# Moving 40 modulation blocks of a two-block transformer kernel: 9 beside the projections, 21 in the attention, 3 behind each of three norms, one behind the first MLP tiles

## The chip, the cores and the metric

One core of a Trainium2 chip. The metric is the device time of one execution in microseconds (us). The five engines are named as in the profile: PE (TensorE, with PEld for its weight loads), DVE (VectorE), ACT (ScalarE), POOL (GpSimd) and SP (SyncE, which here only issues transfers).

## What is computed

The reference runs two blocks on 256 latent tokens (and, in the first block, 256 context tokens) of width 1024, in float32. Only the first block's first two layers matter here. In each of them, for both kinds of tokens:

```python
mod = silu(c) @ w_mod[i] + b_mod[i]          # 6 chunks of 1024, for c and for c_ctx
h = modulate(rms_norm(x, norm1_g[i]), mod[0], mod[1])
x = x + mod[2] * mixer_i(h)                  # differential attention, then neighbourhood attention
x = x + mod[5] * squared_relu_mlp(modulate(rms_norm(x, norm2_g[i]), mod[3], mod[4]), w_mlp1[i], w_mlp2[i])
```

The modulation is one product per layer of a vector pair (the two condition vectors) with a 1024 x 6144 matrix. Behind these two layers come two layers of the second block (gated MLPs, three attention branches, memory attention), which the change leaves as they are.

## The kernel before

**Three passes for each product.** A weight block comes by DMA into one of three slots of `ring`. ACT rounds it to `Wh` and DVE takes the rest `Wl` (`prepare`, lines 1550 and 2076; each in two halves of 128x1024, into one of two buffers), and PE multiplies high by low, low by high and high by high (`passes`, line 806). One step of 128 output rows over 1024 inputs is 24 matmuls. A slot is free for the next transfer once DVE has split it.

**The modulation.** 48 blocks of 1024x256 weights, unsplit. The first 8 (scale and shift of the first norm) are streamed at the start. The other 40 pass through the same ring, 1 MB each, and are used raw: `modulation_block` (line 960) does 8 products with 32 columns of `cT` (shown as 16 records) and accumulates in one PSUM bank, `mod_sum`, which is the last bank of pool A. Here the slot is free once PE has used it. After a group of blocks ACT copies `mod_sum` (`copy_group`), PE folds it (`fold_group`), ACT copies that (`copy_folded`) and DVE adds the bias into `MOD` (`add_group`). Before the change the 40 are placed so: one in each of the 20 steps of layer 0's projections (`first_layer`, `next_modulation(j)`), and 20 in the attention of layer 0, at steps 0, 1, 3, 5 and 6 of every eight (`modulation_step`). Steps are counted from 0; PE does what belongs to step s in its round s + 1.

**The order of transfers** is one list, `blocks`, written in `first_weights`; SP walks through it and waits, for each entry, for the slot of the entry three places back. In layer 0 a projection block is followed by two modulation blocks; after the last projection block come the 20 of the attention, then the four of `a_w_o`. `OUT_SPLITS` has ACT split the first two of these in its rounds 30, 31, 33 and 35 of the attention (32 units, so 35 rounds on PE).

**A norm.** The squares of the 8 tiles of `XT` are summed by POOL and PE; ACT takes a root (lines 1608, 1610), DVE refines it, and then for each of 8 tiles DVE makes `TMP` (line 2167), ACT rounds it to `HTh` (line 1594), DVE takes `HTl` (line 2174), and PE starts on that tile (`side_by_side`: two output tiles at once, 6 matmuls for each k). While that chain starts up, PE has nothing. The weights of the first two output tiles are split long before; of the next block, the first half is split ahead of the norm (`prepare((0,))`) and the second behind it (ACT inside `norm` with `rest=True`, DVE after the 8th tile).

**Pools.** Pool A has PSUM banks pa0 to pa3, pool V pv0 to pv3. A uses three while `mod_sum` is in use: up to the second norm of layer 0. From there it uses four.

**End of the value projections.** The attention's first product waits until the last two value tiles are copied out. In layer 0 the fourth value tile is in pool V and copied by DVE (line 2058), in layer 1 all are in pool A and copied by ACT.

Of the kernel before, what the change touches and what calls it, by code (L numbers as in the profile page):

```python
# [45 lines left out]
QK_MOD = 20  # L46
# [52 lines left out]
def constant_pack():  # L99
# [10 lines left out]
    put("ones", np.ones((P, S)))  # L110
# [17 lines left out]
    put("minus", -np.ones((P, P)))  # L128
# [11 lines left out]
    qc, kc = p % GRID_W, t % GRID_W  # L140
    start = np.clip(qc - NA_COLS // 2, 0, GRID_W - NA_COLS)
    inside = (kc[None, :] >= start[:, None]) & (kc[None, :] < start[:, None] + NA_COLS)
    back = p // GRID_W * GRID_W + GRID_W - 1 - qc
    put("ncol", np.where(inside, 0.0, NEG)[back])
    half = HEAD // 2
    freq = np.power(np.float32(10000.0), -np.arange(half, dtype=np.float32) * np.float32(2.0 / HEAD)).astype(np.float32)
    put("freq", freq[p % half][:, None])
# [6 lines left out]
LATE_CONST = CONST["minus"][0]  # L154
# [159 lines left out]
def program(nc, I, out):  # L314
    ctx = ExitStack()
    with ctx:
# [92 lines left out]
        modtwo = big(12288, 2, 256)  # L409
        cT = big(12800, KT, 64)  # L410
        fold = BIG[:, 13312:13344]
        modt = big(13344, 2, 64)
# [84 lines left out]
        const_late = sem("const_late")  # L497
        mod_in = [sem(f"mod_in{k}") for k in range(KT)]
# [90 lines left out]

        def first_weights(i):  # L590
            w = I["a_w_qkv" if i == 0 else "b_w_qkv"][0]
            if i == 0:
                later = [columns_of_modulation(m) for m in range(LATER_MOD)]
                columns(w, 0, 256)
                for n in range(12):
# [5 lines left out]
                    for src, c in later[2 * n:2 * n + 2] if n < 8 else later[8 + n:9 + n]:  # L601
                        columns(src, c, 256, False)
                for src, c in later[QK_MOD:]:
                    columns(src, c, 256, False)
            else:
                by_columns(w, 0, 2 * D)
                for c in range(2):
                    halves_of_rows(w, 2 * D + c * 512, 512)
            by_columns(I["a_w_o" if i == 0 else "b_w_o"][0], 0, D)
            if i == 1:  # L610
                late_bias.append(len(blocks))
            n = CHUNK * P
            for c in range(FF1 // n + 1):
                if c < FF1 // n:
# [56 lines left out]
        late_bias = []  # L671
# [94 lines left out]
        def _(pe):  # L766
# [342 lines left out]
            def near_attention(tag):  # L1109

                for s in range(len(NEAR_STEPS) + 3):
# [17 lines left out]
                    if s >= 3:  # L1129
# [5 lines left out]
                        for k in range(4):  # L1135
                            for m in range(2):
# [3 lines left out]
                                   v_full if k == 3 and m else None)  # L1140

            def first_layer(i):
                if i == 0:
                    modulation(0)
                else:
                    norm(("n1", i), ALL)
                tiles = qk_tiles(i)
                order = len(tiles)
                for j in range(order + 2):
# [30 lines left out]
                    if i == 0:  # L1180
                        next_modulation(j)
                for n in range(2, 4):
                    values_half(value_tiles(i, 1), CTX_TOKS + LAT_TOKS, 512, n - 2)
                    if i == 0:
                        next_modulation(order + n)
# [34 lines left out]
                if i == 0:  # L1220
                    pe.wait_ge(mod_copied, len(MOD_GROUPS))
                    A.width = BANKS
                norm(("n2", i), tc)
                for c in range(FF1 // P // CHUNK + 1):
# [1659 lines left out]
```

## Time and profile before

| | us |
|---|---|
| median of 3 runs | 2632.49 (2631.89 to 2634.2) |
| profiled execution, its own time | 2634.66 |
| its span | 2632.9 |
| PE busy | 2505.2 (95%) |
| DVE busy | 1702.4 (65%) |
| ACT busy | 1233.6 (47%) |
| POOL busy | 234.2 (9%) |
| mean granted TensorE clock | 0.983 of full |
| mean of DMA | 150 GB/s |

Busy times are of the span. A row of the timeline gives the start, the duration, engine, line, operation, output and inputs, and in brackets the idle time of that engine before it with what ended it. Layer 0 of the first block runs until about 737 us, layer 1 from there to about 1200 us.

### The profile page before, as it was taken

The page shows a single profiled execution, that of the slowest core. Times are in us where ns is not written, and L with a number is a line of the kernel's source. Part 1 is how long each engine was busy: PE and PEld are TensorE (multiplying, and loading weights), DVE is VectorE, ACT ScalarE, POOL GpSimd, SP SyncE. Part 2 cuts the span into 40 slices and gives each one's busy share as a digit, 9 for nine tenths or more (in the row PEclk, how much of TensorE's full clock was granted, in tenths as well). Part 3 has the DMA queues.
Part 4 walks back from the last instruction along what each step waited for, and adds up shares of the span by engine and source line. Part 5 has one row for each costly group of instructions (what it writes and reads, how often), then busy time and mean ns, then how long its engine had stood idle before and what let it go on. Part 6 is the DMA issues. An engine that isn't in the chain of part 4 may idle for free.

```text
span 2632.9 us, 41678 instructions
## 1 busy us (share of the span) xinstructions
PE 2505.2 (95%) x16875; PEld 2220.0 (84%) x16875; DVE 1702.4 (65%) x3155; ACT 1233.6 (47%) x2226; POOL 234.2 (9%) x277
## 2 busy tenths in 40 slices
PE   6999989999989999999999999999999999999998
PEld 4666578888877689999989979899899899798997
DVE  4664855455575566677656777776676567777765
ACT  3443743323255554454444455554544444555543
POOL 1000010000053320000010012000000100120001
PEclk9999999999989999999999999999999999999999
DMA  7655723323235335556555425465765554254654
GB/s 273 201 176 183 234 80 109 97 99 96 96 87 122 81 99 165 172 160 178 168 167 157 149 89 163 141 177 165 199 183 168 167 156 149 88 167 138 177 167 138
DMA packets 497439, 393.74 MB, mean 150 GB/s; under 512 B 26216, under 2 KB 464752, under 8 KB 496352
## 3 DMA queue, kind: packets, MB, share of 16 engines
q1 hardware_dynamic: 494448, 384.92, 48.1%
q0 software_dynamic: 2080, 3.53, 1.1%
q8 instruction: 134, 2.20, 0.4%
q10 hardware_dynamic: 720, 2.62, 0.3%
q14 instruction: 57, 0.47, 0.1%
HBM read 389.99 MB, written 1.05 MB: 149 GB/s over the span
## 4 chain that ended last, share of the span: by engine, by line
PE 82%; DVE 10%; ACT 3%; DMA 2%; issue 2%; POOL 1%; SPq 0%; DVEq 0%; ACTq 0%
PE pv L806 35%; PE pa L806 30%; PE pv L1298 6%; PE pv L771 4%; PE pv L1297 3%; DVE Wl L2076 3%; DMA ring<-in_a_w_qkv_dram 2%; PE pa L771 2%; ACT Wh L1550 2%; PE pa L776 1%; PE pa L960 1%; DVE HTl L2083 0%; POOL BIG L2804 0%; DVE TMP L2167 0%; DVE HTl L2061 0%
## 5 line engine op out<-in xcount | busy, mean ns | idle before, releaser
L2076 DVE TENSOR_TENSOR Wl<-ring,Wh 128x1024 fp32r<-128x1024 f32 (+4 forms) x688 | 758.3, 1143 | 267.9 <-ACT Wh L1550 264.8
L1550 ACT ACTIVATE Wh<-ring 128x1024 fp32r<-128x1024 f32 (+4 forms) x688 | 641.0, 979 | 499.1 <-PE pv L806 329.9
L806 PE MATMUL pa<-HTl,Wh 128*128 128x256 f32 (+1 forms) x1648 | 540.5, 328 | 38.0 <-DVE HTl L2174 24.0
L806 PE MATMUL pv<-HTl,Wh 128*128 128x256 f32 (+1 forms) x1872 | 539.0, 288 | 16.1 <-DVE T L2513 5.8
L806 PE MATMUL pv<-HTh,Wh 128*128 128x256 f32 (+1 forms) x1872 | 537.2, 287 | 0.0
L806 PE MATMUL pv<-HTh,Wl 128*128 128x256 f32 (+1 forms) x1872 | 537.2, 287 | 0.0
L806 PE MATMUL pa<-HTh,Wl 128*128 128x256 f32 (+1 forms) x1648 | 522.2, 317 | 0.0
L806 PE MATMUL pa<-HTh,Wh 128*128 128x256 f32 (+1 forms) x1648 | 521.9, 317 | 0.0
L806 PEld LDWEIGHTS pa<-HTl,Wh 128*128 128x128 f32 x1648 | 320.8, 195 | 72.0 <-issue 45.5
L806 PEld LDWEIGHTS pv<-HTl,Wh 128*128 128x128 f32 x1872 | 359.7, 192 | 21.7 <-issue 12.2
L806 PEld LDWEIGHTS pv<-HTh,Wl 128*128 128x128 f32 x1872 | 359.8, 192 | 2.5
L806 PEld LDWEIGHTS pv<-HTh,Wh 128*128 128x128 f32 x1872 | 359.7, 192 | 2.5
L806 PEld LDWEIGHTS pa<-HTh,Wl 128*128 128x128 f32 x1648 | 320.9, 195 | 20.4 <-issue 1.4
L806 PEld LDWEIGHTS pa<-HTh,Wh 128*128 128x128 f32 x1648 | 320.3, 194 | 18.5
L1298 PE MATMUL pv<-HID,Wh 128*128 128x512 f32 x704 | 246.8, 398 | 0.0
L2743 POOL TENSOR_TENSOR Pb<-Pb 128x256 f32<-128x256 f32 (+1 forms) x60 | 62.6, 1044 | 1453.7 <-ACT Pb L1561 1452.8
L1297 PE MATMUL pv<-HID,Wl 128*128 128x256 f32 x672 | 189.2, 282 | 0.0
L806 PE MATMUL pv<-HID1l,Wh 128*128 128x512 f32 (+1 forms) x512 | 172.0, 336 | 0.0
L806 PE MATMUL pv<-HID1h,Wl 128*128 128x512 f32 (+1 forms) x512 | 172.0, 336 | 0.0
L806 PE MATMUL pv<-HID1h,Wh 128*128 128x512 f32 (+1 forms) x512 | 172.0, 336 | 0.0
L2204 DVE SCALAR_TENSOR_TENSOR XT<-pv,MOD,XT 128x256 f32<-128x256 f32 x216 | 95.7, 479 | 112.0 <-PE pv L806 111.2
L1298 PEld LDWEIGHTS pv<-HID,Wh 128*128 128x128 f32 x704 | 130.4, 188 | 29.4
(288 smaller groups left out, 3307.3 us busy)
## 6 DMA issues: line engine op xcount, KB each, us to landing
ring<-in_ffn_w_gu_dram SPq DMA_DIRECT2D x176, 512.0 KB, 5.1
ring<-in_w_mlp_dram SPq DMA_DIRECT2D x64, 1024.0 KB, 5.4
ring<-in_ffn_w_down_dram SPq DMA_DIRECT2D x64, 704.0 KB, 4.6
ring<-in_w_in_dram SPq DMA_DIRECT2D x42, 1024.0 KB, 5.2
ring<-in_w_mod_dram SPq DMA_DIRECT2D x40, 1024.0 KB, 5.6
ring<-in_a_w_qkv_dram SPq DMA_DIRECT2D x12, 1024.0 KB, 5.3
ring<-in_b_w_qkv_dram SPq DMA_DIRECT2D x12, 1024.0 KB, 5.3
ring<-in_w_out_dram SPq DMA_DIRECT2D x8, 1024.0 KB, 5.1
```

The source lines that it names most:

```text
L771: m = nc.tensor.matmul(o, lhsT=lhsT, rhs=rhs, start=start, stop=stop)
L776: m = nc.tensor.transpose(o, x, C("ident"))
L806: m = nc.tensor.matmul(o, lhsT=x, rhs=y, start=first and j == 0, stop=last and j == 2)
L960: m = nc.tensor.matmul(mod_sum[32 * j:32 * j + 32, 0:256], lhsT=cT[:, k, 30 - 2 * at:62 - 2 * at], rhs=w[:, k, :], start=at == 0 and k < 4 ...
L1297: nc.tensor.matmul(b[:, 0:S], lhsT=wl[:, k, :], rhs=HID2h[:, kk, :], start=False, stop=False)
L1298: m = nc.tensor.matmul(b.rearrange("p (a n) -> p a n", a=2), lhsT=wh[:, k, :], rhs=HID2[:, :, kk, :], start=kk == 0, stop=kk == 2 * half - 1)
L1550: ins = nc.scalar.activation(Wh[rows, p % SPLIT, a:b], ring[rows, i % RING, a:b], ACT.Copy)
L2076: ins = v.tensor_tensor(Wl[rows, p % SPLIT, a:b], ring[rows, i % RING, a:b], Wh[rows, p % SPLIT, a:b].bitcast(F32), ALU.subtract)
L2204: m = v.scalar_tensor_tensor(XT[:, k, half], b[:, at:at + S], MOD[:, i, gate * KT + k, w:w + 1], XT[:, k, half], ALU.mult, ALU.add)
L2743: nc.gpsimd.tensor_tensor(a, a, squares(k)[:, 0:N], ALU.add).then_inc(sum_ready, 1)
```

## The change

Names and line numbers below are those of the new kernel where they are quoted from the diff. It does five things.

1. **Places.** `QK_PLACES` gives 9 modulation blocks to the projections of layer 0 (steps 0, 2, ..., 12, 15, 17, ahead of the rotation product of that step), `modulation_step` now gives 21 to the attention, 3 stand behind the norm product of (n2, 0), of (n1, 1) and of (n2, 1), and the last one behind the first two MLP tiles of layer 1. The list of transfers follows: each trio stands behind the first weight block of its stage.
2. **Splits.** Ahead of those norms nothing of the second weight block is split any more (`last=()`); its first half is split amid the tiles, between the 4th and the 5th, by ACT (`shifted`) and DVE (`normed`), and its second half behind the 8th, by both.
3. **Groups.** Five groups instead of four (8, 16, 8, 12, 4 blocks); the fourth is copied, folded and added in the neighbourhood attention of layer 1, the fifth in the first chunks of its MLP. So `mod_sum` stays in use, and pool A has three banks up to chunk 1 of that MLP. The gains of the last norm are made after the neighbourhood attention.
4. **Value tile.** In layer 1 the fourth value tile is now in pool V too and copied by DVE.
5. **Room.** The small modulation buffers move into the place of late constants; of these, 257 columns are loaded in the projections and 1408 in the MLP of layer 1 (before: 1793 in the projections).

```diff
-QK_MOD = 20
+QK_PLACES = (0, 2, 4, 6, 8, 10, 12, 15, 17)
+QK_MOD = len(QK_PLACES)
+DIFF_MOD = 21
+HOLE_MOD = 3
...
-    return n if QK_MOD <= n < LATER_MOD else None
-MOD_GROUPS = ((0, FIRST_MOD), (FIRST_MOD, 16), (FIRST_MOD + 16, 16), (FIRST_MOD + 32, 8))
-MOD_COPIED = {18: 2, 32: 3}
-MOD_FOLDED = {0: 1, 18: 2, 34: 3}
-MOD_ADDED = {2: 1, 23: 2, 36: 3}
+    return n if QK_MOD <= n < QK_MOD + DIFF_MOD else None
+AFTER_DIFF = QK_MOD + DIFF_MOD
+AFTER_MLP = AFTER_DIFF + HOLE_MOD
+LAST_MOD = AFTER_MLP + HOLE_MOD
+MOD_GROUPS = ((0, FIRST_MOD), (FIRST_MOD, 16), (FIRST_MOD + 16, 8), (FIRST_MOD + 24, 12), (FIRST_MOD + 36, 4))
+MOD_COPIED = {10: 1, 23: 2}
+MOD_FOLDED = {10: 1, 23: 2}
+MOD_ADDED = {15: 1, 28: 2}
+NEAR_COPIED, NEAR_FOLDED, NEAR_ADDED = 2, 4, 6
...
-                    for src, c in later[2 * n:2 * n + 2] if n < 8 else later[8 + n:9 + n]:
-                        columns(src, c, 256, False)
-                for src, c in later[QK_MOD:]:
-                    columns(src, c, 256, False)
+                    for at, place in enumerate(QK_PLACES):
+                        if n == (place // 2 if place < 16 else place - 8):
+                            modulation_columns(at, at + 1)
+                modulation_columns(QK_MOD, AFTER_DIFF)
+                by_columns(I["a_w_o"][0], 0, D)
...
+                elif c == 0:
+                    by_columns(I["w_mlp1"][i], 0, 256)
+                    first = LAST_MOD if i else AFTER_DIFF
+                    modulation_columns(first, first + HOLE_MOD)
+                    by_columns(I["w_mlp1"][i], 256, n)
+                    if i:
+                        modulation_columns(LAST_MOD + HOLE_MOD, LATER_MOD)
...
-            return [(V if i == 0 and t == 3 else A, ("v", i, c, t)) for t in range(4)]
+            return [(V if t == 3 else A, ("v", i, c, t)) for t in range(4)]
...
+                    if i == 0 and j in QK_PLACES:
+                        next_modulation(QK_PLACES.index(j))
                     if j >= 2 and i == 0:
                         pe.wait_ge(qn_ready, seen.more(qn_ready))
...
-                    if i == 0:
-                        next_modulation(j)
...
                 norm(("n2", i), tc)
+                first = LAST_MOD if i else AFTER_DIFF
+                for n in range(first, first + HOLE_MOD):
+                    next_modulation(n)
...
             def shifted(shift, tcols, layer):
                 for k in range(KT):
+                    if k == KT // 2 and (shift, layer) != (0, 0):
+                        prepare((0,))
...
-                    square_block(("o", i), n, 2, tc)
-                norm(("n2", i), tc, RS, 3, layer=i, rest=True)
+                    square_block(("o", i), n, 2, tc, ())
+                norm(("n2", i), tc, RS, 3, layer=i)
+                prepare((1,))
...
-            def normed(terms, shift):
+            def normed(terms, shift, split=True):
                 for k in range(KT + 1):
+                    if k == KT // 2 and split:
+                        prepare((0,))
...
-                for _ in range(4 if i else 1):
-                    prepare()
+                if i:
+                    for _ in range(3):
+                        prepare()
+                    copy_in(value_tiles(i, 0)[3][1], Va[:, 3, 0:512], lambda b: b[:, 0:512])
+                prepare()
+                copy_in(value_tiles(i, 1)[3][1], Va[:, 3, 512:D], lambda b: b[:, 0:512])
```

How this moves instructions, at three places. First, DVE around the second norm of layer 0, before (XT is the residual, T_71 a scratch tile):

```order
L2204 SCALAR_TENSOR_TENSOR XT<-pv,MOD,XT 128x256 x4
L2076 TENSOR_TENSOR Wl<-ring,Wh 128x1024
L2157 SCALAR_TENSOR_TENSOR T_71<-RS 128x512
L2158 SCALAR_TENSOR_TENSOR T_71<-pa,T_71 128x512
L2160 SCALAR_TENSOR_TENSOR RS<-T_71,RS 128x512
L2167 SCALAR_TENSOR_TENSOR TMP<-XT,AM,RS 128x256 x4
L2174 SCALAR_TENSOR_TENSOR HTl<-TMP,MOD,HTh 128x256 x2
L2167 SCALAR_TENSOR_TENSOR TMP<-XT,AM,RS 128x256 x2
```

and now:

```order
L2259 SCALAR_TENSOR_TENSOR XT<-pv,MOD,XT 128x256 x4
L2210 SCALAR_TENSOR_TENSOR T_71<-RS 128x512
L2211 SCALAR_TENSOR_TENSOR T_71<-pa,T_71 128x512
L2213 SCALAR_TENSOR_TENSOR RS<-T_71,RS 128x512
L2222 SCALAR_TENSOR_TENSOR TMP<-XT,AM,RS 128x256 x4
L2229 SCALAR_TENSOR_TENSOR HTl<-TMP,MOD,HTh 128x256 x2
L2222 SCALAR_TENSOR_TENSOR TMP<-XT,AM,RS 128x256 x2
L2229 SCALAR_TENSOR_TENSOR HTl<-TMP,MOD,HTh 128x256 x2
L2222 SCALAR_TENSOR_TENSOR TMP<-XT,AM,RS 128x256 x2
L2229 SCALAR_TENSOR_TENSOR HTl<-TMP,MOD,HTh 128x256 x2
L2129 TENSOR_TENSOR Wl<-ring,Wh 128x1024
L2222 SCALAR_TENSOR_TENSOR TMP<-XT,AM,RS 128x256 x2
```

The half split has moved from ahead of the root to the middle of the tiles, in front of the 5th `TMP` and of the 4th `HTl`. Second, DVE between the last projection step and the first scores (L2313, L2370) of layer 1, before:

```order
L2377 SCALAR_TENSOR_TENSOR BIG<-BIG,gq,RQ 128x512
L2076 TENSOR_TENSOR Wl<-ring,Wh 128x1024 x8
L2313 ISA Lb,mx<-pv,con 128x256
```

and now:

```order
L2436 SCALAR_TENSOR_TENSOR BIG<-BIG,gq,RQ 128x512
L2129 TENSOR_TENSOR Wl<-ring,Wh 128x1024 x6
L2111 COPY BIG<-pv 128x512
L2129 TENSOR_TENSOR Wl<-ring,Wh 128x1024 x2
L2111 COPY BIG<-pv 128x512
L2370 ISA Lb,mx<-pv,con 128x256
```

The two copies of the value tile are new on DVE, and the second stands behind a whole block's split. Third, the last rounds of layer 0's attention on PE, before (con,Pb are the turned probabilities, BIG,PT the products with the values, con,Oa a finished head turned):

```order
L960 MATMUL pa<-ring,BIG 32x256 x8
L776 MATMUL pa<-con,Pb 128x128 x4
L771 MATMUL pa<-BIG,PT 128x128 x4
L776 MATMUL pa<-con,Pb 128x128 x2
L771 MATMUL pa<-BIG,PT 128x128 x4
L776 MATMUL pa<-con,Oa 128x128 x4
L776 MATMUL pa<-con,Pb 128x128 x2
```

and now:

```order
L990 MATMUL pa<-ring,con 32x256 x8
L806 MATMUL pa<-con,Pb 128x128 x4
L801 MATMUL pa<-BIG,PT 128x128 x4
L806 MATMUL pa<-con,Pb 128x128 x2
L801 MATMUL pa<-BIG,PT 128x128 x4
L806 MATMUL pa<-con,Oa 128x128 x4
L990 MATMUL pa<-ring,con 32x256 x8
L806 MATMUL pa<-con,Pb 128x128 x2
```

There is one modulation block more, in PE's round 33, and so each of the `a_w_o` blocks stands one place later in the list of transfers.

## Rows read from the trace of the kernel before

**Rows 1.** Chain that ended last, 62 to 97 us: start, us, what.
```profile
57.90 5.76 DMA ring<-in_a_w_qkv_dram
...
63.68 2.01 ACT Wh L1550 x2
...
71.60 1.87 PE pa L960 x16
73.46 7.21 PE pa L806 x24
...
81.53 0.43 PE pv L771 x2
81.96 1.00 PE pa L960 x16
82.96 5.67 PE pa L806 x24
```

**Rows 2.** Timeline of PE: its waits at the places of the change.
```profile
70.38 1.22 PE L771 MATMUL pv<-BIG,con 128*128 128x256 f32 x2 [3.01 <-DVE BIG L2377]
...
184.46 1.22 PE L771 MATMUL pv<-BIG,con 128*128 128x256 f32 x2 [4.65 <-DVE BIG L2377]
...
326.22 1.16 PE L771 MATMUL pa<-BIG,PT 128*128 128x128 f32 x8 [1.25 <-ACT PT L1627]
...
385.15 0.76 PE L806 MATMUL pa<-HTl,Wh 128*128 128x512 f32 x1 [6.48 <-DVE HTl L2174]
...
744.83 0.55 PE L806 MATMUL pa<-HTl,Wh 128*128 128x256 f32 x1 [5.90 <-DVE HTl L2174]
...
880.34 1.13 PE L771 MATMUL pv<-BIG 64*128 64x512 f32 x4 [0.89 <-ACT BIG L1627]
...
968.78 0.55 PE L806 MATMUL pa<-HTl,Wh 128*128 128x256 f32 x1 [4.43 <-DVE HTl L2174]
```

**Rows 3.** Timeline of DVE, end of layer 0's value projections.
```profile
235.25 0.69 DVE L2058 COPY BIG<-pv 128x512 f32<-128x512 f32 x1 [20.36 <-PE pv L806]
```

**Rows 4.** Timeline of SP and ACT near the end of layer 0's attention.
```profile
319.59 0.37 SPq L2843 DMA_DIRECT2D ring<-in_a_w_o_dram  x1
...
322.00 1.05 ACT L1550 ACTIVATE Wh<-ring 128x1024 fp32r<-128x1024 f32 x1
```

**Rows 5.** DMA issues, 300 to 330 us: count, KB each, median us to landing.
```profile
ring<-in_a_w_o_dram SPq DMA_DIRECT2D x4, 1024.0 KB, 5.2
```

**Rows 6.** Timelines of ACT and DVE, second norm of layer 0.
```profile
387.66 0.91 ACT L1594 ACTIVATE HTh<-TMP,MOD 128x256 fp32r<-128x256 f32 x2 [0.80 <-DVE TMP L2167]
...
389.25 0.88 DVE L2174 SCALAR_TENSOR_TENSOR HTl<-TMP,MOD,HTh 128x256 fp32r<-128x256 f32 x2
...
396.42 1.23 DVE L2076 TENSOR_TENSOR Wl<-ring,Wh 128x1024 fp32r<-128x1024 f32 x1
...
398.25 0.60 ACT L1627 ACTIVATE XQ<-pa 128x512 f32<-128x512 f32 x1 [2.85 <-PE pa L806]
```

**Rows 7.** Timelines around the norms of layer 1: DVE, SP, ACT, DVE, ACT.
```profile
751.97 1.23 DVE L2076 TENSOR_TENSOR Wl<-ring,Wh 128x1024 fp32r<-128x1024 f32 x1
...
960.46 0.37 SPq L2843 DMA_DIRECT2D ring<-in_w_mlp_dram  x1
...
970.11 0.51 ACT L1594 ACTIVATE HTh<-TMP,MOD 128x256 fp32r<-128x256 f32 x1 [0.41 <-DVE TMP L2167]
...
974.90 1.23 DVE L2076 TENSOR_TENSOR Wl<-ring,Wh 128x1024 fp32r<-128x1024 f32 x1
...
976.90 0.38 ACT L1627 ACTIVATE XQ<-pa 128x256 f32<-128x256 f32 x1 [2.62 <-PE pa L806]
```

**Rows 8.** Stretch 890 to 932: PE, PEld, DVE, ACT, POOL busy, PEclk, DMA share, GB/s.
```profile
890.00:932.00 42.00, 41.28 (x352) 25.94 (x350) 34.77 (x149) 32.38 (x77) 21.76 (x29) 0.97 0.28 44
```

**Rows 9.** Timeline of DVE behind layer 1's value projections.
```profile
881.06 2.36 DVE L2076 TENSOR_TENSOR Wl<-ring,Wh 128x1024 fp32r<-128x1024 f32 x2 [8.94 <-ACT Wh L1550]
```

**Rows 10.** Timeline of ACT in layer 1's attention: the copies of turned probabilities.
```profile
900.83 1.06 ACT L1627 ACTIVATE SQ<-pa 128x512 f32<-128x512 f32 x2
```

More of the change, by code:

```diff
@@ L109, in constant_pack @@
     put("ident", np.eye(P))
-    put("ones", np.ones((P, S)))
+    put("ones", np.ones((P, P)))
     put("block", (p[:, None] // HEAD == p[None, :] // HEAD) * 1.0)
@@ L126, in constant_pack @@
     put("eps", np.full((P, 1), EPS))
-    put("minus", -np.ones((P, P)))
+    t = np.arange(S)
+    qc, kc = p % GRID_W, t % GRID_W
+    start = np.clip(qc - NA_COLS // 2, 0, GRID_W - NA_COLS)
+    inside = (kc[None, :] >= start[:, None]) & (kc[None, :] < start[:, None] + NA_COLS)
+    back = p // GRID_W * GRID_W + GRID_W - 1 - qc
+    put("ncol", np.where(inside, 0.0, NEG)[back])
+    half = HEAD // 2
+    freq = np.power(np.float32(10000.0), -np.arange(half, dtype=np.float32) * np.float32(2.0 / HEAD)).astype(np.float32)
+    put("freq", freq[p % half][:, None])
     pb = np.zeros((P, P))
@@ L408, in program, with spare @@
         posi = over("posi", [P, S], where["BIG"] + 4 * 12032, I32)
[L409 to L412, printed above, removed]
+        def spare(at, tiles, width):
+            return con[:, LAST_CONST + at:LAST_CONST + at + tiles * width].rearrange("p (t n) -> p t n", n=width)
+        modtwo = spare(0, 2, 256)
+        cT = spare(512, KT, 64)
+        modt = spare(1024, 2, 64)
+        fold = con[:, LAST_CONST + 1152:LAST_CONST + 1184]
         MODW = over("MODW", [P, 2048], where["SQ"])
@@ L497, in program @@
         const_late = sem("const_late")
+        const_last = sem("const_last")
         mod_in = [sem(f"mod_in{k}") for k in range(KT)]
@@ L588, in columns_of_modulation, with modulation_columns @@
             return I["w_mod"][layer], n * 256
+        def modulation_columns(m0, m1):
+            for m in range(m0, m1):
+                src, c = columns_of_modulation(m)
+                columns(src, c, 256, False)
         def first_weights(i):
@@ L1146, in first_layer @@
                     norm(("n1", i), ALL)
+                    for n in range(AFTER_MLP, LAST_MOD):
+                        next_modulation(n)
                 tiles = qk_tiles(i)
@@ L1232, in first_layer @@
                             linear(A, ("up", i), c * CHUNK + j, (0, P), ht(tc), N, c == 0 and j == 0)
+                            if i and (c, j) == (0, 0):
+                                for n in range(LAST_MOD + HOLE_MOD, LATER_MOD):
+                                    next_modulation(n)
+                        if i and c == 1:
+                            fold_group(4)
+                            A.width = BANKS
                     if c:
@@ L1573, in square_block @@
                         square(k, tcols, (key, k))
-                    prepare(last)
+                    if last:
+                        prepare(last)
                 else:
@@ L1734, in first_layer @@
                 else:
-                    norm(("n1", i), ALL, RS, 0, mean=PT[:, 1, :], layer=i, rest=True)
+                    norm(("n1", i), ALL, RS, 0, mean=PT[:, 1, :], layer=i)
+                    prepare((1,))
                 tiles = qk_tiles(i)
@@ L1801, in first_layer @@
                             rounded(HID1h[:, c % 2, j, 0:N], TMP[:, j % 2, 0:N])
+                        if i and c == 0:
+                            copy_group(4)
+                        if i and c == 1:
+                            copy_folded(4)
                     if c == FF1 // P // CHUNK and i == DEPTH - 1:
@@ L2182, in norm_mod @@
                          RS[:, half.start - tcols.start:half.start - tcols.start + S]) for half, w in halves(tcols)],
-                       lambda k, half: MOD[:, i, 3 * which * KT + k, (half != LAT):(half != LAT) + 1])
+                       lambda k, half: MOD[:, i, 3 * which * KT + k, (half != LAT):(half != LAT) + 1], key != ("n1", 0))
             def normed_quarters(tcols, gain, r, at, tiles=range(KT)):
@@ L2207, in residual_gated @@
                     if (k + 1) % per_block == 0:
-                        prepare(last if k == KT - 1 else (0, 1))
+                        parts = last if k == KT - 1 else (0, 1)
+                        if parts:
+                            prepare(parts)
             def residual(keys, factor, tiles=range(KT), per_block=0):
@@ L2355, in first_layer @@
                 else:
-                    gains(1, 0, 1)
+                    gains(1, 0)
                     v.tensor_copy(gq[:, 5:6], gq[:, 4:5]).then_inc(am_ready, 1)
@@ L2401, in first_layer @@
                     near_attention(("att", i))
+                    gains(1, 1)
                     N, tc = S, LAT
-                residual_gated(lambda k: (("o", i), k), i, 2, tc, 2, last=(0,))
+                residual_gated(lambda k: (("o", i), k), i, 2, tc, 2, last=())
                 norm_mod(("n2", i), tc, 1, i)
@@ L2419, in first_layer @@
                             rest(HID1h[:, c % 2, j, 0:N], HID1l[:, c % 2, j, 0:N], t)
+                        if i and c == 1:
+                            add_group(4)
                     if c == FF1 // P // CHUNK and i == DEPTH - 1:
@@ L2425, in first_layer @@
                         residual_gated(lambda k: (("dn", i, c - 1), k), i, 5, tc, 4,
-                                       last=(0,) if c == FF1 // P // CHUNK else (0, 1))
+                                       last=() if c == FF1 // P // CHUNK else (0, 1))
             def scaled(name, l, k):
```

55 lines of the change are left out of this document (29 added, 26 removed).

## Prediction

> **What bounds the kernel now.** The table of engines comes first: PE is busy for 2505.2 of 2632.9 us, DVE for 1702.4. So the time is PE's work plus its 128 us of waits, and an instruction elsewhere counts only where PE waits for it. The chain that ended last says it again: nearly all of its time is on PE [rows 1]. In it one modulation block is 1.00 us of PE where the clock is full, and 1.87 behind a wait. The list of PE's waits shows where the change could act [rows 2]: 3.01 in the second projection step, 4.65 in the third pair, 1.25 near the end of layer 0's attention, and 6.48, 5.90 and 4.43 at the three norms. The timelines of DVE, ACT and SP say what ends each wait [rows 3, 4, 6, 7, 9, 10].
>
> The 40 blocks cost PE 40 us in either kernel. The change can gain only where a block falls into a wait of PE, and where something is late no more; and it can lose where the new order makes something late.
>
> **The change part by part**, against the profiled execution (2634.66).
>
> 1. *Projections.* 20 blocks become 9: 11 x 1.00 = -11.0 [rows 1].
> 2. *First wait.* The chain runs through a weight transfer issued at 57.90 only, because its slot comes free behind two modulation blocks; it takes 5.76, ACT's rounding 2.01, and PE waits 3.01 for DVE's query tile behind that [rows 1, 2]. Then PE works at half clock: 1.22 for 0.43, 1.87 for 1.00, 7.21 for 5.67, together 3.2 more [rows 1, 2]. With one modulation block between two weight blocks instead of two, that weight block takes the slot of a weight block which DVE has split long before, so it lands in time. -3.0 and -3.2, so -6.2. Bounds: -6.2 and 0 (the query's own chain of copies stays). I take the whole, since the transfer is the last thing that ended.
> 3. *Second wait.* The 4.65 at 184.46 [rows 2] is the root and the product of the last query tile, behind which PE has nothing queued in either order: 0.
> 4. *End of the value projections.* The modulation block of the last step covered DVE's copy of a value tile (0.69, done at 235.94) [rows 3]. PE now stands at it: +0.9 with the handing over. Bounds 0.7 to 1.0.
> 5. *Attention.* The 21st block stands in PE's round 33, next to the wait of 1.25 at 326.22 [rows 2]: between 0 (it fills it) and +1.0; one fold with its copy and sum has left the attention (ACT and DVE time, bounds -0.8 and 0). I take 0 for both together.
> 6. *The output weights.* They stand one place later in the list of transfers. The first output block gets the place that the second has now, issued at 319.59 [rows 4]. Landing takes 5.2 [rows 5], so it is there at 324.8, and ACT wants the first block at 322.00, in front of copies that PE waits for: +2.8. PE's clock falls in a wait of such length, as in part 2 (where 3.01 brought 3.2): I take +1.2, since part of the wait lies in one that is there already. Bounds for the two together: 0 (ACT gets there later too) and 2.8 + 3.2 = 6.0; I take 4.0. The Trainium skill, "DMA: Bandwidth & Descriptors", section "Anatomy of one DMA — SWDGE (gpsimd) path", gives about 2.0 us and the bytes by 436 GB/s, so an estimated 4.4 us for 1 MB, for another issuing path than SP's; by that the wait would be 2.0 and the sum 0.8 lower. The row has 5.2, and the sum goes by the row.
> 7. *Norms, the blocks.* Three blocks are 3.0 us of PE, and the waits are 6.48, 5.90 and 4.43 [rows 2]. The loads are early: at the last norm the third block's slot comes free where now a weight block is issued at 960.46 [rows 7], and with 5.2 it has landed at 965.7, while PE, whose wait begins at 968.78 - 4.43 = 964.35, comes to the third block at 966.4. So 9 blocks for 0, bounds 0 and +2. The last one, behind the first MLP tiles, is in the open: +1.0.
> 8. *Norms, the split.* Ahead of the norm the half split was covered by the wait. Amid the tiles it isn't: at (n2, 0) ACT ends the 4th `HTh` at 388.57, the half `Wh` takes 1.05 [rows 4], then the half `Wl` 1.23, until 390.9, where DVE takes the next `TMP` now ahead of the 4th `HTl` of 389.25, at about 388.4 [rows 6]. So the tiles behind come 2.5 later, the 8th at 398.9 instead of 396.4 (the end of the last `HTl` is where `Wl` starts now). PE was some 1.0 behind there (it ends the first output tile at 398.25, three matmuls into the 8th tile, while DVE had ended at 396.4), so +1.6. At (n2, 1) DVE ended at 974.90 and the first output tile at 976.90 [rows 7]: PE was 1.2 or so behind, +1.5. There the second weight block may land just when ACT wants it (the 4th `HTh` ends at 970.6), bounds 1.0 and 2.7. At (n1, 1) I have no such lag, +1.9. Together +5.0, bounds 3 and 7.
> 9. *Layer 1's value tiles.* The second copy (0.69) on DVE stands behind a block's split that now starts at 881.06 and takes 2.36 [rows 9], so it ends near 883.9, if the split starts where it does now, 0.3 sooner if not. PE starts at 880.34 [rows 2], but what waits in fact is DVE: its first scores come behind the same split already, and are 0.7 of copy and some handing over later. I take +1.5, bounds 0.7 and 3.6 (all of 883.9 - 880.34).
> 10. *Fourth group* in the neighbourhood attention: PE's fold and DVE's sums, +0.7, bounds 0 and 1.5; PE is busy 41.28 of 42 us there [rows 8]. Its copies are on ACT, busy 32.38 of 42: 0.
> 11. *At nothing:* the fifth group, the gains made later and the late constants' transfer lie beside PE's work in the MLP; their cover is DVE's and ACT's idle fifth. Pool A with three banks was enough for layer 0. If that cover is gone, see rival 3.
>
> Sum: -11.0 - 6.2 + 0.9 + 0 + 4.0 + 1.0 + 5.0 + 1.5 + 0.7 = **-4.1**, so 2630.6 against 2634.66. That execution was 2.2 above the median of the three runs, so against the median 2628.4; I say 2628.5.
>
> A measurement of this kernel can tell about 0.2%, 5.3 us. So the likeliest case is, narrowly, no change that can be told.
>
> **Rivals.**
>
> 1. *As summed*, -4: each uncertain term near its value. For it: each has a row. The sum lies near the limit of what can be told.
> 2. *The new waits are shorter than summed* (faster). In part 6 ACT may come to the split later than at 322.00, since the 21st block and later copies push it, and then nothing waits: -4.0. In part 8 the tile chain could be absorbed more at the last norm; in part 9 only the lower bound may hold, -0.8. Together -9 or so: 2623.5. Against it: the slot's time in part 6 is tied to PE's use of modulation blocks, which would be later too.
> 3. *Pool A with three banks* (slower). In layer 1's attention PE's products of a step take banks of pool A while ACT copies the turned probabilities out, 2 copies in 1.06 us [rows 10]. With one bank less the product of a step must wait for a copy of the step before. I see about 0.4 us of slack now. The stretch is 16 steps and PE has no reserve there (41.28 of 42) [rows 8]: from 0.25 us a step on it outweighs the gain of 4.1, and a whole copy (0.53) and its handing over, 1.0 less the slack, would be 16 x 0.6 = +9.6: then 2638.1, just slower by what can be told (2637.8). For it: ACT's 32.38 of 42. Against it: layer 0 lives with three.
> 4. *The first wait stays* (the change does not do there what it says). If the query tile is late for another reason than the transfer (the three steps of copy, root and product behind PE's own work), 6.2 stay: +2.1, 2634.7 against the median. Against it: at 63.68 ACT's rounding waits for the transfer, and nothing else ends there.
>
> **How the numbers follow.** As summed, no change that can be told, 0.40; faster by more than 5.3 us (rival 2, and the part of case 1 that falls beyond the limit) 0.42; rival 4 0.09, told as the same; rival 3 0.09. So faster 0.42, same 0.49, slower 0.09. The range takes in rival 2 with part 8 at its lower bound (2621), case 1 and rival 4 with a little above (2636): what is left out is rival 3 and some of the best cases. Between faster and same the profile does not decide much; I give the value of the sum, 2628.5.
>
> **What will show it.** In the list of PE's waits: the 3.01 of the second projection step gone and the stretch of 72 to 82 us at full clock (part 2, rival 4); a wait of about 0.9 at the end of the value projections (4); one of some 3 us near round 30 of the attention, ended by ACT behind a transfer (6; rival 2 if it isn't there); at the norms waits of 3.5, 3 and 1.5 us behind three blocks instead of 6.48, 5.90 and 4.43 (7), and new ones in the middle of the tiles, on the 5th tile's `HTl`, of 1 to 2 us (8); before layer 1's attention a gap of over 0.89 ended by DVE's copy (9); in that attention waits of the products for `SQ` copies, once per step (rival 3). Granted clock below 0.9 in stretches without a wait ahead of them would upset all of this. I am wrong in kind if PE's busy time changes by more than the fold and the clock explain, or if the time at the norms falls by 3 us each.

## The result, and the profile after

The changed kernel takes 2641.71 us (median of 7 executions, 2637.8 to 2643.55), the kernel before 2633.3 in the same comparison (7 executions). The ratio is 1.0027 [1.0018, 1.0037]: it is slower, where no change that can be told was forecast, and outside the range (2621 to 2636). The profiled execution is the shortest of the seven, 3.9 us under their median: 2637.8, span 2636.0. Busy times have hardly moved: PE 2505.3 (2505.2 before), DVE 1704.1, ACT 1232.2, POOL 238.7 (234.2 before).

PE's timeline at the places of [rows 2] (start, duration, engine, line, operation, in brackets the wait ahead and what ended it):

```profile
168.10 1.22 PE L801 MATMUL pv<-BIG,con 128*128 128x256 f32 x2 [4.42 <-DVE BIG L2436]
216.51 1.99 PE L801 MATMUL pv<-BIG 64*128 64x512 f32 x8 [0.99 <-DVE BIG L2111]
308.63 1.65 PE L801 MATMUL pa<-BIG,PT 128*128 128x128 f32 x6 [2.91 <-ACT PT L1672]
371.52 0.47 PE L836 MATMUL pa<-HTl,Wh 128*128 128x512 f32 x1 [3.75 <-DVE HTl L2229]
378.86 0.50 PE L836 MATMUL pa<-HTl,Wh 128*128 128x512 f32 x1 [1.32 <-DVE HTl L2229]
733.38 0.35 PE L836 MATMUL pa<-HTl,Wh 128*128 128x256 f32 x1 [3.58 <-DVE HTl L2229]
739.17 0.39 PE L836 MATMUL pa<-HTl,Wh 128*128 128x256 f32 x1 [1.38 <-DVE HTl L2229]
873.34 2.08 PE L801 MATMUL pv<-BIG 64*128 64x512 f32 x4 [4.40 <-DVE BIG L2111]
960.64 0.36 PE L836 MATMUL pa<-HTl,Wh 128*128 128x256 f32 x1 [1.34 <-DVE HTl L2229]
966.50 0.50 PE L836 MATMUL pa<-HTl,Wh 128*128 128x256 f32 x1 [3.14 <-DVE HTl L2229]
```

All that was looked for is there: no wait in the second projection step (the granted clock of 72 to 82 us is 1.00, before 0.77), 0.99 at the end of the value projections, 2.91 near the end of the attention, the three holes down to 3.75, 3.58 and 1.34, a second wait amid the tiles of each norm, and 4.40 ahead of layer 1's attention. So the places tell nothing of a loss. To find it, lay the same matmul of both traces side by side and take the difference of its starts (of its ends, where the row says "end"). That is PE's lead (negative: the changed kernel is ahead):

| place (before, after) | lead |
|---|---|
| first attention's same product (239.68, 219.84) | -19.8 |
| head norm at its end (333.99, 320.29) | -13.7 |
| first tile of (n1, 1) (744.83, 733.38) | -11.5 |
| end of layer 1's value products (879.45, 868.94) | -10.5 |
| end of that attention (938.62, 930.85) | -7.8 |
| end of an output block amid layer 1's MLP (1030.08, 1026.33) | -3.8 |
| 1367.19, 1362.43 | -4.8 |
| 1570.82, 1567.04 | -3.8 |
| 1707.29, 1706.60 | -0.7 |
| 2623.91, 2626.76 | +2.9 |

Up to 1367 us the changed kernel is ahead by about what the sum gave (-4.1). All is lost in the second block, which the change leaves as it is: 1.0 us up to 1571, 3.1 between 1571 and 1707, 3.5 in the rest. What differs there is on POOL, in its products with `before`, a mask of zeros and ones, 512 columns wide, in the constants `con`. First the kernel before, then the changed one: its groups with this mask (busy, mean ns of one), and PE's waits for them (us in total, times, longest):

```profile
L2809 POOL TENSOR_TENSOR TMP<-TMP,con 128x512 f32<-128x512 f32 x10 | 11.2, 1120 | 9.0 <-ACT TMP L1939 8.9
L2804 POOL TENSOR_TENSOR BIG<-BIG,con 128x512 f32<-128x512 f32 x10 | 10.9, 1092 | 388.8 <-DVE BIG L2604 388.8
...
PE pv L771 <- POOL BIG L2804: 9.1, 8, 1.8
```

```profile
L2874 POOL TENSOR_TENSOR TMP<-TMP,con 128x512 f32<-128x512 f32 x10 | 13.1, 1307 | 10.2 <-ACT TMP L1992 10.2
L2869 POOL TENSOR_TENSOR BIG<-BIG,con 128x512 f32<-128x512 f32 x10 | 12.7, 1267 | 389.4 <-DVE BIG L2669 389.4
...
PE pv L801 <- POOL BIG L2869: 11.5, 10, 2.1
```

PE behind the last of these waits in this part of the block, and behind a wait for DVE 50 us later, which is equally long in both; before, then after:

```profile
1570.82 1.56 PE L771 MATMUL pv<-BIG,con 128*128 128x256 f32 x6 [1.54 <-POOL BIG L2804]
1620.78 0.36 PE L806 MATMUL pv<-HTl,Wh 128*128 128x256 f32 x1 [2.70 <-DVE T L2513]
```

```profile
1567.04 2.64 PE L801 MATMUL pv<-BIG,con 128*128 128x256 f32 x6 [1.72 <-POOL BIG L2869]
1618.60 0.55 PE L836 MATMUL pv<-HTl,Wh 128*128 128x256 f32 x1 [2.70 <-DVE T L2578]
```

And PE's clock behind both (columns as in [rows 8]), before and after:

```profile
1570.00:1580.00 10.00, 9.18 (x63) 8.24 (x63) 4.66 (x8) 2.04 (x5) 2.90 (x3) 1.00 0.28 80
1618.00:1640.00 22.00, 19.30 (x161) 19.25 (x161) 19.99 (x34) 12.95 (x23) 7.22 (x7) 1.00 0.54 175
```

```profile
1566.00:1578.00 12.00, 10.96 (x64) 9.71 (x65) 4.85 (x9) 2.25 (x5) 3.50 (x3) 0.86 0.22 68
1618.00:1638.50 20.50, 19.90 (x153) 19.93 (x154) 17.04 (x29) 11.97 (x21) 4.82 (x5) 0.92 0.56 172
```

The same 20 products take 0.18 us more each. The change drops 256 columns of constants ahead of the mask and moves the 256 of `ncol` and the single column `freq` there, so the mask starts at column 1667 of `con`, not 1666. This is part 5 of the change (its "room"), on which the prediction has no word but "at nothing".

### The profile page after: what moved, and what is told of

The parts are those of the page before. It is cut to its first block, busy times and chain, and to the rows that moved or that the text cites. A ratio compares the mean times of both kernels' runs of the same rounds, so it can differ in the third digit from the quotient of the medians.

```text
span 2636.0 us, 41703 instructions
## 1 busy us (share of the span) xinstructions
PE 2505.3 (95%) x16879; PEld 2222.1 (84%) x16879; DVE 1704.1 (65%) x3161; ACT 1232.2 (47%) x2226; POOL 238.7 (9%) x277
## 4 chain that ended last, share of the span: by engine, by line
PE 84%; DVE 9%; ACT 3%; DMA 2%; issue 2%; POOL 1%; SPq 0%; DVEq 0%; ACTq 0%; POOLq 0%
PE pv L836 35%; PE pa L836 30%; PE pv L1340 6%; PE pv L801 4%; PE pv L1339 3%; DVE Wl L2129 3%; PE pa L801 2%; ACT Wh L1592 2%; PE pa L806 1%; DMA ring<-in_a_w_qkv_dram 1%; PE pa L990 1%; POOL BIG L2869 0%; DVE HTl L2136 0%; DVE TMP L2222 0%; DVE Lb L2372 0%
```

## Experiments

Medians of before are of the executions made beside each kernel. Two kernels that were not run side by side can be compared by their medians or by their ratios to before; where the two differ, both are given. "Lead" is read as above, against the profiled execution of before, and each trace is one execution.

### 1. The mask's column

```diff
 put("freq", ...)
+put("gap", np.zeros((P, 1)))          # f1_even; 2 columns in f2_odd2
```

> The changed kernel with one column of zeros put behind the single column `freq`, so that all constants behind it, the mask `before` among them, start at an even column again (1668; 1667 in the changed kernel, 1666 before). Nothing is reordered. Theory A (odd columns): GpSimd reads the mask slower from an odd column, 1.27 us an operation instead of 1.09; its ten longer waits and the clock that falls behind them in the second block are what turned a gain of 4.7 us at 1360 us into a loss of 3. Then the operations take 1.09 here, PE is 4 to 5 us ahead of the kernel before at 1360 and stays so to the end: about 2628.5, 0.18% faster than before. Theory B (the place): the mask is slow because of where it and its neighbours lie, not because of the odd column: 1.27 stays, and so does the time, 2638 to 2642. Theory C (the phase): the operations are at 1.09 but PE's clock falls in the second block all the same, because every wait there comes 4.7 us earlier than before: 2634 to 2640.

> As f1_even, but with two columns of zeros: the mask starts at column 1669, odd again, and lies 8 bytes behind its place in the changed kernel. Theory A: the operations with the mask take 1.27 us as in the changed kernel, time 2636 to 2643. Theory B: a move by any amount could mend it, 1.09 us. The pair of this run and f1_even tells oddness from place.

f1_even, mask at 1668: 2640.95 against 2633.52, ratio 1.0028 [1.0016, 1.0041], the products still at 1.27 us. f2_odd2, mask at 1669: 1.09 us, and 2631.89 in its only execution. So theory A's half on odd and even is wrong, and theory B's in its first form too: a column decides, by another rule.

```diff
 put("minus", -np.ones((P, P)))        # kernel before
+put("gap", np.zeros((P, 1)))
```

> The kernel before, with one column of zeros ahead of `halves`, so that the mask `before` starts at column 1667 as in the changed kernel; the order of the work is untouched. Theory A: the ten operations go from 1.09 to 1.27 us, the ten waits of PE for POOL from 9.1 us to about 11.5, and the clock falls behind some of them: 2636 to 2641, slower than before by 0.15 to 0.3%, all of it behind 1500 us. Theory C: the operations are slower, but only 10 x 0.2 = 2 us reach the time, 2635, and the granted clock of the second block is as before. Theory B: no slower operation, 2633.

f3_before_odd, the old order with the mask at 1667: 2642.47, ratio 1.0033 [1.002, 1.0046]. One column of zeros costs the kernel before 9 us. Its products, its waits and its clock in the two stretches are those of the changed kernel:

```profile
L2805 POOL TENSOR_TENSOR BIG<-BIG,con 128x512 f32<-128x512 f32 x10 | 12.7, 1266 | 389.3 <-DVE BIG L2605 389.3
...
PE pv L772 <- POOL BIG L2805: 11.5, 10, 2.1
...
1570.00:1580.00 10.00, 9.24 (x55) 8.60 (x56) 4.43 (x8) 0.90 (x2) 3.22 (x3) 0.83 0.21 63
1618.00:1640.00 22.00, 19.30 (x150) 19.13 (x149) 18.44 (x28) 12.16 (x20) 7.02 (x7) 0.92 0.48 160
```

Only 2.4 us of the loss are waits for the mask. The rest is PE at half clock, behind such waits and behind others that are no longer than before.

```diff
+put("gap", np.zeros((P, 2)))
 put("before", ...)                    # changed kernel
```

> The changed kernel with two columns of zeros ahead of the mask `before` alone, which moves from column 1667 to 1669 (where f2_odd2 had it); `halves`, `later` and `upto` stay where the change puts them. If the mask is the one constant whose place counts, GpSimd's ten pairs of products with it take 1.09 and 1.12 us, PE's waits for them 9.1 us in all, and the time is 2630 to 2632.5, faster than before by about 0.1%. If the other constants behind it count (PE's products with `halves`), the time stays at 2638 to 2642 although GpSimd is fast.

g2_mask2: 2634.41 against 2632.92, ratio 1.0006 [0.9997, 1.0014]; products at 1.09, waits 9.2 us. Of the constants, `halves`, `later` and `upto` don't count: 7.3 us less than the changed kernel by the medians, 5.5 by the ratios. (`ncausal`, which DVE reads, lies behind the mask and moved with it; its maxima over 128x256 take 0.42 us in either kernel.) But the time is above what was expected. Freed of the mask, the change gives nothing that can be told, where 4 us were forecast. In g2's trace the lead is -3.0 at 1030 us and 0.0 at 1168; 3 us go in a stretch with equal waits (2.92 and 2.55, as before) and clock 0.97, where before has 0.99. The traces of f1_even, f3_before_odd, g3_probe and i1_slowmask lose 3 us there too, those of the changed kernel, f2_odd2 and the others do not. f2_odd2 does the same work as g2_mask2, with the mask at the same column, so this term may well come and go between executions; no kernel was traced twice, and no run here settles what decides it.

```diff
+for at in (0, 1):
+    for o in range(1636, 1668):
+        t = (TMP, SQ)[tried % 2] (flat)[:, at:at + 512]
+        nc.gpsimd.tensor_tensor(t, t, con[:, o:o + 512], ALU.mult)
```

> The changed kernel with 64 products on GpSimd behind the end of all other work: scratch of 128x512 by 512 columns of the constants that start at column 1636, 1637, ... 1667, one after the other; first with the scratch at an aligned address, then with it 4 bytes further. Other engines are idle. If the column alone sets the speed, the durations fall into two groups, 1.09 and 1.27, and repeat with some period in the column; columns 1666 and 1667 are then apart by 0.18. If it takes another engine's traffic at the same time to make the difference, all 32 durations of a kind are equal. The whole time is about 75 us longer by construction.

Columns 1636 to 1640 with the scratch at its own start, then 1636 to 1639 with the scratch one column further (g3_probe, POOL's timeline):

```profile
2641.30 1.26 POOL L2891 TENSOR_TENSOR TMP<-TMP,con 128x512 f32<-128x512 f32 x1 [14.09 <-DMA out_dram<-BIG]
2642.64 1.09 POOL L2891 TENSOR_TENSOR SQ<-SQ,con 128x512 f32<-128x512 f32 x1
2643.81 1.09 POOL L2891 TENSOR_TENSOR TMP<-TMP,con 128x512 f32<-128x512 f32 x1
2644.98 1.26 POOL L2891 TENSOR_TENSOR SQ<-SQ,con 128x512 f32<-128x512 f32 x1
2646.32 1.26 POOL L2891 TENSOR_TENSOR TMP<-TMP,con 128x512 f32<-128x512 f32 x1
...
2681.49 1.26 POOL L2891 TENSOR_TENSOR TMP<-TMP,con 128x512 f32<-128x512 f32 x1
2682.83 1.27 POOL L2891 TENSOR_TENSOR SQ<-SQ,con 128x512 f32<-128x512 f32 x1
2684.18 1.09 POOL L2891 TENSOR_TENSOR TMP<-TMP,con 128x512 f32<-128x512 f32 x1
2685.35 1.09 POOL L2891 TENSOR_TENSOR SQ<-SQ,con 128x512 f32<-128x512 f32 x1
```

The pattern has a period of four columns (16 bytes) over all 64 products: with the scratch at a multiple of four columns, remainders 1 and 2 take 1.09 and remainders 0 and 3 take 1.26. With the scratch moved by one column, the fast ones are 2 and 3. The kernel places `con` and both scratch tiles at multiples of 32 bytes. So what counts is the distance of the two operands in columns, modulo 4, and no other engine need be at work. 1666 and 1669 (remainders 2 and 1) are fast, 1667 and 1668 (3 and 0) slow, as in the four kernels.

### 2. The first wait

```diff
 # kernel before, list of transfers
-w0, w1, M0, M1, w2, M2, M3, w3, ...
+w0, w1, M0, w2, M1, M2, M3, w3, ...
```

> The kernel before with two entries of the list of transfers exchanged: the third projection block now stands ahead of the second modulation block, so its slot is one that comes free early. The order of the work on every engine is untouched. If the first wait (3.01 us at 67.4) and the half clock behind it (3.2 us) are this transfer alone, both go: -6.2, time 2627, and nothing else in the trace moves except in time. Rival: the second modulation block now comes late (its slot is freed with the second weight block's split) and PE waits for it a step earlier: 2631 to 2634. The prediction's rival 4 (the query tile is late for another reason): 2633.

g1_early: 2634.44 against 2632.92, ratio 1.0005 [0.9996, 1.0014]. The rival holds: the wait has changed its name, and at 95 us PE is 0.35 later than before. The wait now:

```profile
63.71 1.93 PE L965 MATMUL pa<-ring,BIG 128*32 128x256 f32 x16 [4.03 <-DMA ring<-in_w_mod_dram]
```

```diff
-QK_PLACES = (0, 2, 4, 6, 8, 10, 12, 15, 17)     # on g4_nomid, below
+QK_PLACES = (0, 1, 4, 6, 8, 10, 12, 15, 17)
```

> g4_nomid (2626.7) with the 9 blocks of the projections at steps 0, 1, 4, 6, ... instead of 0, 2, 4, 6, ..., and the list of transfers to match: again two modulation blocks between the second and the third projection block. PE's work and its order but for that block are the same. If the first transfers set the pace (g1_early: either the weight block or the modulation block is late), a wait of 3 to 4 us comes back ahead of 70 us, with half clock behind it, and the time is 2626.7 + 3 to 6.2: 2630 to 2633. Rival: with fewer blocks behind it the start catches up, below 1 us: 2627.

h2_places: 2631.23 against 2626.74 without the edit, and the wait is back under its old name:

```profile
70.70 0.76 PE L802 MATMUL pv<-BIG,con 128*128 128x256 f32 x2 [3.51 <-DVE BIG L2433]
```

PE's lead at 179.80 us of before is -10.3 here and -16.0 in g4_nomid, 5.7 apart: one block of 1 MB more in the list ahead of the third projection block costs that. Before, in g1_early and in h2_places, two blocks are wanted by 67 us: the third weight block, at which ACT stands ahead of the query tile's root, and the second modulation block. One of them is issued at 41 us and the other only at 58, when a slot is free. The changed kernel wants that modulation block a step later.

### 3. The value tile, and the split amid the tiles

```diff
-                prepare()
+                if i == 0:
+                    prepare()
                 copy_in(value_tiles(i, 1)[3][1], Va[:, 3, 512:D], ...)
+                if i:
+                    prepare()
```

> The changed kernel, but in layer 1 DVE copies the fourth value tile's second half ahead of the split of the next weight block instead of behind it. If the 4.40 us wait of PE at 868.94 is the split (it waits for ACT's rounding, which starts when the value products end, 2.0 us, and takes 2.36 us itself), the wait falls to about 1.0 us, the one of 2.0 us for the first maxima comes back as it was before, and PE is 2 to 3 us further ahead at the end of that attention (10 us ahead of before instead of 7.8). Rival: the first scores on DVE then wait for the split and give all of it back, 7.8 stays. The whole time also holds what happens in the second block, so the reading is at 930 us.

> g2_mask2 (2634.4) with f4_swap's edit alone, so that g4_nomid (2626.7) comes apart into its two edits. From the traces of g2 and g4, PE loses 2.8 us from the end of layer 1's value products to the end of its attention in g2 and 0.7 in g4, so the swap is worth 2.1 us and the split moved out of the tiles the other 5.6: then 2632 to 2632.5 here. Rival: the swap takes most of it, since an earlier start keeps PE's clock up: 2629 or less. Other rival: it is worth nothing by itself: 2634.

f4_swap, one execution: 2639.68, lead -7.5 at the end of the attention. At 755 us it was 1.7 us behind the changed kernel (lead -7.6 against -9.3), and 0.2 behind at the attention's end: 1.5 gained. h1_mask2swap, the same edit on g2_mask2: 2633.09, ratio 0.9994 [0.9985, 1.0003], less than g2_mask2 by 1.3 by the medians and 3.2 by the ratios, near the limit of what can be told. Its lead goes from -11.6 to -10.4 over that attention, where g2's goes from -9.8 to -7.1: 1.7 us. f4_swap's expectation (2 to 3) was too high: PE's wait falls from 4.40 to 0.99 as expected, but 1.50 comes back as a wait for the first maxima. h1_mask2swap ended 0.6 above its range.

```diff
 for k in range(KT):                   # ACT's shifted, DVE's normed alike
-    if k == KT // 2 ...:
-        prepare((0,))
 ...
-prepare((1,))                         # behind the 8th tile
+prepare()
```

> g2_mask2 with two edits more. First, f4_swap's. Second, nothing is split amid the normed tiles any more: ACT and DVE split both halves of the second weight block behind the 8th tile. My reading is that the split in the middle delays tiles 5 to 8 by 2.5 us and PE by 1.3 to 3.1 us at each of the three norms. Then these waits (1.33, 1.38, 3.14 us) go, but the two output tiles that need the split stand behind PE's first two: ACT's 2.0 and DVE's 1.2 come at once behind the 8th tile, PE has about 1 us of work left there, and a wait of about 2 to 2.5 us takes the place of each. So within 1 us of g2_mask2 less what the swap gives (1.4): 2629 to 2631. Rival: the block that lands late at (n2, 1) is hidden now, and 2 us more are saved: 2627. Other rival: the new waits are 3 us and more each, and it is slower than g2_mask2: 2632 to 2634.

g4_nomid: 2626.74 against 2632.92, ratio 0.9977 [0.9968, 0.9986], faster than both kernels. The waits amid the tiles (1.50, 1.88 and 3.13 in h1_mask2swap) are gone, and what I put in their place hardly comes. Behind the 8th tile there are a new wait of 0.56 at (n2, 0), none at (n1, 1), and this at (n2, 1):

```profile
965.24 0.39 PE L837 MATMUL pa<-HTl,Wh 128*128 128x256 f32 x1 [0.85 <-DVE Wl L2128]
```

Against h1_mask2swap this is 6.4 us by the medians and 4.5 by the ratios. Against my "within 1 us" it is a miss, and the time is that of the first rival (2627). But its reason, the late block at (n2, 1), is only part: by the leads across each norm's tiles the three give 1.4, 2.3 and 3.5 us. PE still waits for both halves of the block (`split_slot`). They come sooner than the 3.2 us that I counted, since ACT starts to round them while DVE is at the last tile: DVE ends its last `HTl` at 383.20 and the second half at 385.63, 2.4 later (2.8 at (n2, 1)). And PE ends its first two output tiles 1.9 us behind that `HTl`, not 1; at (n2, 1) the last modulation block, which stands there, makes it 2.0.

### 4. The output weights

```diff
-OUT_SPLITS = {30: 0, 31: 1, 33: 0, 35: 1}       # on g4_nomid
+OUT_SPLITS = {31: 0, 32: 1, 34: 0, 35: 1}
```

> g4_nomid with the splits of the first two output blocks in ACT's and DVE's rounds 31, 32, 34 and 35 instead of 30, 31, 33 and 35. In g4 ACT stands 2.61 us at the transfer of the first output block, and PE 2.70 behind it. One round later (3 us) the block is there. If the wait is that transfer alone: the 2.70 goes, 2624. Rival: the splits, now closer together, delay ACT's copies in rounds 32 to 35, and PE waits as long a little later: 2626 to 2627.5.

In the changed kernel, ACT's timeline shows the wait of part 6:

```profile
307.04 1.06 ACT L1592 ACTIVATE Wh<-ring 128x1024 fp32r<-128x1024 f32 x1 [2.81 <-DMA ring<-in_a_w_o_dram]
```

h3_outsplits: 2620.48 against 2633.27, ratio 0.9951 [0.9939, 0.9964], 13 us faster than before, and 3.5 below the 2624 that the wait alone would give. PE's waits there are what they were before the change or less:

```profile
309.34 1.16 PE L802 MATMUL pa<-BIG,PT 128*128 128x128 f32 x8 [1.26 <-ACT PT L1671]
...
313.37 0.71 PE L802 MATMUL pa<-BIG,PT 128*128 128x128 f32 x4 [0.61 <-ACT PT L1671]
```

3.6 us of the 6.3 are gained by the end of the attention (lead -13.2 in g4_nomid, -16.8 here, at 378.08 us of before), the clock of 270 to 340 us going from 0.95 to 1.00. Another 2.6 come between 745 and 880 us, with no edit there; why is not shown.

### 5. The mask once more

```diff
-put("gap", np.zeros((P, 2)))          # on h3_outsplits: mask back at 1667
 put("before", ...)
```

> h3_outsplits (2620.5) with the mask `before` back at column 1667, where the change puts it. In the probe a column decides over 1.09 or 1.26 us by its remainder by 4. If the slow mask costs what it cost in the other two arrangements (7.3 us from g2_mask2 to the changed kernel, 9 from before to f3_before_odd), through PE's ten longer waits (2.4 us) and the clock that falls behind them, the time is 2627 to 2629.5. If the loss of clock there hung on the instant at which the second block starts (this kernel reaches it 12 us earlier than before), only the 2.4 us of waits come back: 2623.

i1_slowmask: 2626.72, ratio 0.9975 [0.9966, 0.9984] where h3_outsplits has 0.9951: 6.2 us, with PE's waits for POOL back at 11.5. That is 0.3 below the expected range, and far from the 2.4 us of the waits alone. In three arrangements the column is worth 7.3, 9 and 6.2 us by the medians, 5.5, 8.7 and 6.3 by the ratios. The traces agree: from 1367 us to the end, PE loses 7.2 to 8.0 us against before in all six with the mask at a slow column, and 0.1 to 4.4 in the seven with it at a fast one.

## Why the prediction was wrong

The step that failed is part 11, "at nothing", for the constants. It looked at when the late constants are transferred, not at where they then lie. That they move by a column is in the diff; that the operand's place is a cost was in no row I had read, and PE's waits for POOL in the second block (9.1 us) were not looked at, because the change "leaves them as they are". This term is +7.3 by the medians, +5.5 by the ratios (changed kernel against g2_mask2), and makes slower what would have been no change that can be told. It is not the whole miss: from 2628.5 to 2641.7 are 13.2 us, and the other 6 stay where the mask is fast (g2_mask2, 2634.4). None of the rivals was it: rival 3, the one on the slow side, did not come (in the attention with three banks PE waits only twice for a copy into `SQ`, 0.17 us each, not once per step), and rival 4 did not either.

The other steps, by the trace:

- *Parts 1 to 4, projections.* Forecast -16.3; the lead goes from -0.3 at the first tile to -19.8 in the first attention, so -19.5. The wait and its half clock went as said. A modulation block costs more than its 1.00 [rows 1]: two steps take 15.93 us with two blocks (90.85 to 106.78 before) and 14.73 with one (96.34 to 111.07 after), so 1.20 each, 2.2 more for eleven; the last 1.0 of the difference I can't place. The mechanism of part 2 was half right. The transfer is what PE waits for, but not because it stands at the wrong place in the list; in g1_early, with the same blocks in another order, PE waits for the modulation block instead (4.03 us). That the third weight block takes a slot that is free early (issued at 41.1 us, before at 57.90) helps only since a block less is asked for.
- *Parts 5, 6.* Forecast 0 and +4.0; measured +6.1 over the attention. ACT's wait is 2.81 (forecast 2.8) and removing it gives 3.6 with the clock (4.0). The other 2.5 are the 21st block (1.2), which I had put at nothing, and a wait of 1.30 at 284.62 for ACT's copy of a finished group, whose step the regrouping moved. The transfer took 5.3 (forecast 5.2). By the estimate of 4.4 from the Trainium skill, "DMA: Bandwidth & Descriptors", section "Anatomy of one DMA — SWDGE (gpsimd) path", the wait would have been 2.0: for SP's path the measurement decides.
- *Part 7.* The nine blocks fit the holes: 6.48, 5.90 and 4.43 became 3.75, 3.58 and 1.34, and PE's first product behind them runs at full clock (0.47, 0.35 and 0.36 us, before 0.76, 0.55 and 0.55), though at the first two norms the clock is at half about 1 us later.
- *Part 8.* Forecast 1.6, 1.9 and 1.5 for the split amid the tiles. From the first tile of (n2, 0) to that of (n1, 1) the lead falls by 2.2. At (n2, 1), with the last block's 1.0, it falls by 4.0 instead of 2.5: the second weight block landed late (ACT waits 0.80 for it), and PE waits 3.14. With the 1.0 the bound was 3.7. Within (n1, 1) it falls by 2.1 (forecast 1.9); by the end of the value products 1.2 of this has come back, where the kernel before has more half clock. Taken out, the split is worth 6.4 with the clock (g4_nomid).
- *Parts 9, 10.* Forecast +1.5 and +0.7; measured +2.7 for both together, with no row that parts them. PE's gap of 4.40 is 1.2 until the first half is rounded, 2.3 of DVE's split, 0.7 of the copy and 0.2 of handing over, and 3.5 more than before: the forecast's upper bound of 3.6, not its 1.5. The overlap was wrong. Before, PE made its first scores beside the split, so that DVE's first maximum came 3.9 us behind the value products (883.34); now these scores too stand behind the copy, and it comes 6.6 behind (875.53), 2.7 later.

The sum of these at 1030 us was -3.8 against a forecast of -4.1 for the whole: close, though by errors of both signs. And it is one execution's: in g2_mask2, without the mask's loss, the median gain is none. In its trace the lead is -3.0 at 1030 us, and 3.0 are lost between 1030 and 1100, where PE's clock falls in some traces and not in others; what decides it stays open.

## What to carry to other kernels

Compare the traces at the same instruction along the whole span before explaining anything: here the change's own places were right, and the loss lay 500 us behind the last edit. When a diff moves data in memory, list every operation that reads what moved; a place can cost like an instruction. And a block moved into a hole pulls its transfer with it: ask what the ring delivers later (the first output block, the second MLP block), and move the work that waits for it. Four edits, these splits (g4_nomid, h3_outsplits), the value tile's copy and the mask's column, turned 1.0027 into 0.9951.

## What the runs showed of the hardware

- GpSimd's product of two float32 operands (128x512, from SBUF) takes 1.09 or 1.26 us by the distance of their start addresses modulo 16 bytes: fast at 4 and 8 bytes, slow at 0 and 12, with nothing else running (64 products). Two operands that are both aligned are a slow pair. The Trainium skill, "SBUF — State Buffer", section "Operand start alignment", says which starts are legal and that its runs timed nothing; the probe adds the time.
- A small wait can cost more than itself. 0.18 us on twenty products, 2.4 us of PE's waits, came to 6 to 9 us, because the granted clock went to half more often (0.83 to 0.92 over 10 to 22 us where it was 1.00): behind a mask wait of 1.72 us where 1.54 had kept it, and also behind a wait of 2.70 us for DVE that is as long in the kernel before, where the clock stayed at 1.00. So the length of the wait ahead does not alone decide; what does, no run here settles. The Trainium skill, "TensorE: Matmul & The Clock Gate", section "What's actually happening", says that the throttled state is the default and that activity releases it; the traces agree in that the half clock of these stretches stands behind waits of PE. They don't tell which waits: behind 2.09 us (1558.67 in the changed kernel) the clock was still whole.
